# Streaming both halves of the activations in one 512-column matmul, and a new order of the first layer's projections

## The chip, the cores and the metric

The kernel runs on one core of one Trainium2 chip. The metric is the device time of one execution in microseconds (us); "before" and "after" are compared as medians of several executions. TensorE (PE) multiplies, ScalarE (ACT) and VectorE (DVE) prepare operands and drain results, GpSimd (POOL) and SyncE (SP) issue transfers.

## The reference, cut to what matters

The input is `x` of 256 rows by 2048 columns in float32. Three layers follow each other:

```python
h = rmsnorm(x, attn_norm[0]); p = h @ even_w_in[0]        # 2048 x 6144
qa, ka, va, qb, kb, vb = split(p, 6 * [1024])
# A: 8 heads of 128, relative-position bias;  B: 4 heads with two maps each, out = (p0 - lam * p1) @ v, rmsnorm
x = x + concat(A, B) @ even_w_out[0];  x = x + ffn(rmsnorm(x), 0)
h = rmsnorm(x, attn_norm[1]); p = h @ odd_w_in[0]          # queries 2048, latent 256, index queries 512, index key 64, 8 weights
# C: index scores pick 64 keys per row; 16 heads attend over them through the latent
x = x + C @ odd_w_out[0];  x = x + ffn(rmsnorm(x), 1)
# third layer: a convolution branch, windowed attention, gates, w_out_2, layer norm
```

All of it is float32. The products are made with float32r operands split in two: a high part (a rounded copy) and a low part (the rest). Of the four partial products three are computed: high x high, high x low, low x high.

## The kernel before, in words

**Units and groups.** Every weight matrix is read in *units* of 512 KB (4 tiles of 128 rows by 256 columns, or 2 tiles by 512 columns in a "wide" unit). For each unit SP issues one transfer into a ring of four buffers `raw`; ACT makes the high part (`hi`, L190, instruction L195), DVE the low part (`lo`, L197, instruction L201), both into `ws`; PE multiplies. Some units make a *group*, which accumulates into two PSUM banks of `PG`; groups alternate between banks 0,1 and banks 2,3. `Seg` (L42) numbers units and groups of a stage. The semaphore `s_mm` counts finished units, `s_drain` drained groups.

**Three ways to multiply a unit.** `mul_T` (L215) gives transposed results: the weights are stationary and the activations `hs` (high part at `[.., 0, :]`, low part at `[.., 1, :]`, 256 columns each, side by side in memory) stream; a unit is 4 x 2 triples of 256-column matmuls, 24 instructions, all recorded at L223. Queries, keys and the index products of the second layer use it. `mul_N` (L227) gives natural results: the activations are stationary, 256 columns of weights stream; 24 instructions at L234. The values of the first layer and one group of the third use it. `mul_W` (L238) does the same with 512 columns of weights in a wide unit: 12 instructions at L245. Everything else uses it.

**Who does what in which order.** There is no scheduler. `group_pe` (L248) is PE's side of a group: it waits for the bank (`s_drain`), then for each unit waits for `lo`, multiplies, and after unit j runs `hooks[j]`. `group_side` (L264) is the side of ACT and of DVE: for each unit j the hook `("early", j)`, at the last unit the drain of the group, then `hi` or `lo` for the unit four places ahead (which waits until PE has finished unit j), then the hook j. Attention is spread over these hooks by hand, so each engine runs a fixed list, and a wait in it holds back all that is behind it on that engine.

**The first layer.** `even` (L870) is called for A (`gA`) and B (`gBs`), each 12 groups of 4 units: for each of four pairs j of heads a query group, a key group (both `mul_T`) and a value group (`mul_N`). The steps of pair j run in the hooks of the next three groups (`hooks`, L955): scores `S_` on PE (L791, L792), `max_` on DVE (`maxima`, L795, instructions L806 to L809), `exps` on ACT (L817), `soft` on DVE (L890; A: L827, B: L894 to L902), the turn `T_` on PE (L834), `pt_` on ACT (L845), the product with the values `V_` on PE (L854, L855). B goes on with `b_sq` (ACT, L919), `b_st` (PE, L923 and L924), `b_a` (DVE, L615), `rstd_act` (ACT), `b_on` (DVE, L626 to L629 and L932), `b_hi` (ACT, L937) and `b_lo` (DVE, L943). The steps of B's last pair run in the hooks of the first group of the output projection `gEO` (L1013). Its last units wait for B's last tiles.

**Drains.** `scaled_drain` (L371) is one DVE instruction (L377, or L381 where the rows are turned round) from PSUM, scaled by 1/rms, into `qst`, `kst` or `qi`.

**The second layer.** `gI` (L1088) has four groups: index key, latent, two of index queries; `score` (L1040) on PE follows from its fourth group on, `c_norm` (L1126) on DVE lies in the third. `gU` (L1157) makes keys and values from the latent; `gQ` (L1277) makes the 16 heads' queries in eight groups of 4 units. Over `gU` and the first groups of `gQ` DVE runs eight rounds of `top` (L1061), then `selection`; POOL then adds the masks, DVE does `c_max`, ACT `exps`, DVE `norms` (L827), and PE's `flips` (L834) of the first heads come after the first unit of `gQ`'s third group.

Of the kernel before, what the change touches and what calls it, by code (L numbers as in the profile page):

```python
# [30 lines left out]
UK = 4  # L31
# [37 lines left out]
def build(nc, a):  # L69
# [30 lines left out]
    vst1 = at("vst1", [P, 2, S], F32, o1 + 49152 + 1536)  # L100
    cs = at("cs", [P, 2, 2, S], F32R, o1 + 53248)
# [395 lines left out]
    def setup_act(e):  # L497
# [16 lines left out]
        w(e, "nat", 1)  # L514
# [198 lines left out]
    def ffn(p, seg, segd, l, before_seg, norm, own, pn, gain):  # L713
# [4 lines left out]
        cross_before = {"f0": 0, "f1": 19}[p]  # L718
# [130 lines left out]
    def mix(e, p, j, v, free, pt=lambda h: pT[:, h, :]):  # L849

        w(e, p + "pT", j + 1)
        free()
        for h in (0, 1):
            e.matmul(PO[:, h, 0:S], v(0, h), pt(h)[:, 0:S], start=True, stop=False)  # L854
            ins = e.matmul(PO[:, h, P:S], v(1, h), pt(h)[:, S:384], start=False, stop=True)  # L855
        ins.then_inc(sem(p + "O"), 1)
# [13 lines left out]
    def even(seg, p, c0, before):  # L870

        is_b = p == "B"
        k_of = [0, 1]

        def S_(e, pp, j):
            sg = gA if pp == "A" else gBs
            if pp == "B":
                w(e, "BD", 5 * j)
            scores(e, pp, j, lambda h: qst[:, 0, h, :], lambda h: kst[:, h, :],
                   lambda: e.wait_ge(s_drain, sg.group(0, 3 * j + 1) + 3))  # L880
# [52 lines left out]

        def b_hi(e, j):
            w(e, "Bon", j + 1)
            for h in (0, 1):
                e.activation(os_[:, bass.ds(8 + 2 * j + h, 1), 0, :], sqb[:, h:h + 1, :], ACT.Copy, scale=gB[:, h:h + 1]).then_inc(sem("Boh"), 1)  # L937

        def b_lo(e, j):
            w(e, "Boh", 2 * j + 2)  # L940
            for h in (0, 1):
                t = bass.ds(8 + 2 * j + h, 1)
                e.scalar_tensor_tensor(os_[:, t, 1, :], sqb[:, h:h + 1, :], gB[:, h:h + 1], os_[:, t, 0, :].bitcast(F32), ALU.mult, ALU.subtract).then_inc(sem("Bos"), 1)  # L943

        def start_hooks(name, e):

            return {k: hooked(e, v) for k, v in {
                "pe": {0: {0: lambda e: (x_pe(e, 2), tables_pe(e)), 1: lambda e: x_pe(e, 3)}, 1: {0: lambda e: (w(e, "tabD", 3), spread_pe(e, "n0"))}, 2: {1: lam_pe}},
                "act": {0: {0: lambda e: squares(e, "n0", 3), 1: lambda e: norm_act(e, "n0")}, 2: {2: lam_act}},
                "dve": {0: {0: lambda e: (norm_first(e, "n0"), lines_second(e)), 1: lambda e: (norm_second(e, "n0"), spread_diag(e, "n0")),  # L950
                            ("late", 3): lambda e: spread_copy(e, "n0")},
                        2: {3: lambda e: lam_dve(e)}}}[name].items()}


        def hooks(name, e, pp, j):  # L955
            A = {"pe": {0: {0: lambda: S_(e, pp, j)}, 1: {0: lambda: T_(e, pp, j), 2: lambda: V_(e, pp, j)}},
                 "act": {0: {1: lambda: exps(e, pp, j)}, 1: {0: lambda: pt_(e, pp, j), 3: lambda: out_hi(e, pp, j, 2 * j)}},
                 "dve": {0: {0: lambda: max_(e, pp, j), 2: lambda: soft(e, pp, j)}, 1: {3: lambda: out_lo(e, pp, j, 2 * j)}}}
            B = {"pe": {0: A["pe"][0], 1: A["pe"][1], 2: {0: lambda: b_st(e, j)}},
                 "act": {0: A["act"][0], 1: {0: lambda: pt_(e, pp, j), 2: lambda: b_sq(e, j)},  # L960
                         2: {0: lambda: rstd_act(e, "B", j), 3: lambda: b_hi(e, j)}},
                 "dve": {0: A["dve"][0], 2: {("early", 1): lambda: b_a(e, j), 1: lambda: b_on(e, j), 3: lambda: b_lo(e, j)}}}
            return (A if pp == "A" else B)[name]
# [1022 lines left out]
```

## Time and profile before

| | |
|---|---|
| median of 3 executions | 2540.35 us (2539.18 to 2540.77) |
| the profiled execution, its own time | 2539.02 us |
| its span, first to last instruction | 2536.8 us |
| PE busy | 2512.4 us, 99%, 13171 matmuls |
| DVE busy | 1441.6 us, 57% |
| ACT busy | 1181.5 us, 47% |
| mean granted TensorE clock | 0.998 |
| read from HBM | 459.63 MB, 182 GB/s over the span |

The profile page gives the busy time of each engine, the span in 40 slices, the chain of work that ended last and the costliest groups of instructions. Matmuls overlap in the pipeline, so the "mean ns of one" of a matmul is longer than its share of the time; the share is read from the chain, where a run of n matmuls has its duration. The time outside the span is 2539.02 - 2536.8 = 2.2 us.

### The profile page before, as it was taken

To read this page: it belongs to the slowest core of one execution; us is meant where nothing else is said; L and a number is where in the kernel's file an instruction comes from. 1 tells how busy PE (TensorE), PEld (TensorE's weight loads), DVE (VectorE), ACT (ScalarE), POOL (GpSimd) and SP (SyncE) were. 2 spreads that over 40 slices of the span, in tenths; PEclk is the share of its full clock that TensorE was granted. 3 is DMA by queue.
4 is the path that set the end of the run, shared out by engine and by line. 5 is a ranking of instruction groups with operands and counts; after the bars stand their busy time and mean duration, and the time that the engine had idled before them with its cause. 6 is when DMAs were issued, how large, how long until landed. Compare 5 with 4: busy or idle time off the path is not lost.

```text
span 2536.8 us, 34992 instructions
## 1 busy us (share of the span) xinstructions
PE 2512.4 (99%) x13171; PEld 2154.9 (85%) x13171; DVE 1441.6 (57%) x1967; ACT 1181.5 (47%) x1543; POOL 50.1 (2%) x71
## 2 busy tenths in 40 slices
PE   9999999999999999999999999999999999999997
PEld 9999988888888888889998888888888888888776
DVE  6555555544544544446765554554554444798875
ACT  5344455444444444444444544444444444545763
POOL 1000000000000000000120000000000000000000
PEclk9999999999999999999999999999999999999999
DMA  7555555656556655546544566656655555655453
GB/s 230 171 171 171 166 174 181 194 189 189 188 189 187 189 191 191 191 167 208 162 142 168 179 195 189 188 187 190 189 189 192 190 191 191 219 183 162 147 181 133
DMA packets 291477, 463.31 MB, mean 183 GB/s; under 512 B 17343, under 2 KB 115825, under 8 KB 290858
## 3 DMA queue, kind: packets, MB, share of 16 engines
q1 hardware_dynamic: 288960, 453.63, 55.1%
q0 software_dynamic: 1792, 8.11, 1.0%
q8 instruction: 73, 1.20, 0.2%
q14 instruction: 34, 0.28, 0.0%
q10 hardware_dynamic: 618, 0.09, 0.0%
HBM read 459.63 MB, written 2.14 MB: 182 GB/s over the span
## 4 chain that ended last, share of the span: by engine, by line
PE 95%; DVE 2%; ACT 2%; issue 1%; DMA 0%; DVEq 0%; SPq 0%; ACTq 0%
PE PG L245 73%; PE PG L223 12%; PE PG L234 4%; PE PS L729 1%; DVE ws L201 1%; PE PS L568 1%; PE PS L791 1%; PE PO L854 1%; ACT ws L195 1%; PE PS L834 0%; PE PG L1170 0%; PE PO L1179 0%; DVE cacc L1401 0%; PE PO L855 0%; PE PS L792 0%
## 5 line engine op out<-in xcount | busy, mean ns | idle before, releaser
L201 DVE TENSOR_TENSOR ws<-raw,ws 128x1024 fp32r<-128x1024 f32 x860 | 1055.8, 1229 | 1022.4 <-ACT ws L195 1018.0
L195 ACT ACTIVATE ws<-raw 128x1024 fp32r<-128x1024 f32 x860 | 910.3, 1060 | 1206.5 <-PE PG L245 948.0
L245 PE MATMUL PG<-ws,hs 128*128 128x512 f32 x5184 | 1191.3, 390 | 0.0
L245 PEld LDWEIGHTS PG<-ws,hs 128*128 128x128 f32 x5184 | 969.2, 188 | 200.5
L245 PE MATMUL PG<-ws,fs 128*128 128x512 f32 x2112 | 481.3, 389 | 0.0
L245 PEld LDWEIGHTS PG<-ws,fs 128*128 128x128 f32 x2112 | 395.9, 188 | 81.9
L223 PE MATMUL PG<-hs,ws 128*128 128x256 f32 x2640 | 331.3, 285 | 0.4 <-issue 0.3
L223 PEld LDWEIGHTS PG<-hs,ws 128*128 128x128 f32 x2640 | 320.7, 192 | 1.9 <-issue 1.0
L245 PE MATMUL PG<-ws,os 128*128 128x512 f32 x1152 | 267.9, 392 | 2.0 <-DVE ws L201 1.3
L245 PEld LDWEIGHTS PG<-ws,os 128*128 128x128 f32 x1152 | 214.7, 188 | 47.9 <-DVE ws L201 3.2
L234 PE MATMUL PG<-ws,hs 128*128 128x256 f32 x864 | 106.6, 284 | 0.0
L234 PEld LDWEIGHTS PG<-ws,hs 128*128 128x128 f32 x864 | 104.9, 192 | 0.2
L1401 DVE SCALAR_TENSOR_TENSOR cacc<-hc,convw,cacc 128x256 f32<-128x256 f32 x232 | 98.0, 479 | 0.0
L817 ACT ACTIVATE ts<-ts,small 128x256 f32<-128x256 f32 x96 | 42.4, 443 | 23.4 <-DVE small L809 23.4
L757 ACT ACTIVATE cross<-PG,small 128x512 f32<-128x512 f32 x44 | 27.9, 686 | 33.2 <-PE PG L245 33.2
L770 DVE SCALAR_TENSOR_TENSOR qst<-PG,small,cross 128x512 f32<-128x512 f32 x44 | 31.0, 747 | 10.5 <-PE PG L245 10.5
L559 DVE SCALAR_TENSOR_TENSOR hs<-PS,gains,hs 128x256 fp32r<-128x256 f32 x72 | 29.8, 477 | 4.3 <-ACT hs L552 4.3
L552 ACT ACTIVATE hs<-PS,gains 128x256 fp32r<-128x256 f32 x72 | 28.0, 471 | 5.8 <-PE PS L585 5.8
L738 DVE TENSOR_TENSOR fs<-PS,fs 128x1024 f32 (+1 forms) x22 | 26.8, 1218 | 0.0
L545 ACT ACTIVATE cross<-x 128x512 f32<-128x512 f32 x40 | 25.3, 634 | 2.9 <-DVE x L708 0.3
L729 PEld LDWEIGHTS PS<-ident,qst 128*128 128x128 f32 x176 | 20.5, 140 | 2.9
L708 DVE TENSOR_TENSOR x<-x,PG 128x1024 f32<-128x1024 f32 x16 | 19.5, 1220 | 5.9 <-PE PG L245 5.9
(264 smaller groups left out, 832.0 us busy)
## 6 DMA issues: line engine op xcount, KB each, us to landing
raw<-in_w_gate SPq DMA_DIRECT2D x176, 512.0 KB, 4.3
raw<-in_w_up SPq DMA_DIRECT2D x176, 512.0 KB, 3.5
raw<-in_w_down SPq DMA_DIRECT2D x176, 512.0 KB, 3.4
raw<-in_even_w_in SPq DMA_DIRECT2D x96, 512.0 KB, 3.5
raw<-in_w_in SPq DMA_DIRECT2D x52, 512.0 KB, 3.4
raw<-in_odd_w_in SPq DMA_DIRECT2D x44, 512.0 KB, 3.5
raw<-in_even_w_out SPq DMA_DIRECT2D x32, 512.0 KB, 3.5
raw<-in_odd_w_out SPq DMA_DIRECT2D x32, 512.0 KB, 3.4
```

Source lines behind the costliest of these rows:

```text
L195: e.activation(ws[j % RING][:, :, 0, :], raw[:, j % RING], ACT.Copy).then_inc(s_hi, 1)
L201: e.tensor_tensor(w[:, :, 1, :], raw[:, j % RING], w[:, :, 0, :].bitcast(F32), ALU.subtract).then_inc(s_lo, 1)
L223: ins = e.matmul(PG[:, bank + c, 0:S], w_, x_, start=first and kk == 0 and n == 0, stop=last and kk == UK - 1 and n == 2)
L234: ins = e.matmul(PG[:, bank + b, 0:UC], x_, w[:, kk, h, :], start=first and kk == 0 and n == 0, stop=last and kk == UK - 1 and n == 2)
L245: ins = e.matmul(out[:, b, :], x_, w[:, kk, :, h, :], start=first and kk == 0 and n == 0, stop=last and kk == 1 and n == 2)
L552: e.activation(hs[:, n, 0, :], src(t), ACT.Copy, scale=gains[:, gain, n:n + 1]).then_inc(sem(p + "hi"), 1)
L559: e.scalar_tensor_tensor(hs[:, n, 1, :], src(t), gains[:, gain, n:n + 1], hs[:, n, 0, :].bitcast(F32), ALU.mult, ALU.subtract).then_inc(se ...
L729: ins = e.transpose(turned[:, t, b * P:(b + 1) * P], nat_f[:, b, t * P:(t + 1) * P], ident[:])
L757: ins = e.activation(sil[:, b], gates[:, b, :], ACT.Silu, scale=rnT[:, b:b + 1])
L770: ins = e.scalar_tensor_tensor(nat_f[:, b], ups[:, b, :], rnT[:, b:b + 1], sil[:, b], ALU.mult, ALU.mult)
L817: e.activation(ts[:, h, src], ts[:, h, src], ACT.Exp, bias=nmx[:, n:n + 1], accum_out=sm[:, n:n + 1]).then_inc(sem(p + "e"), 1)
L1401: e.scalar_tensor_tensor(dst, hc[:, n, c:c + S], convw[:, n, c:c + 1], dst, ALU.mult, ALU.add).then_inc(sem("cv"), 1)
```

## The change

It has five parts.

1. `mul_T` streams high and low part of the activations together: per tile and column block one matmul of 512 columns with the high weights, one of 256 columns with the low weights, in place of three of 256.
2. The high x low part now lies in columns 256 to 511 of the bank. So the drain of such a group is three steps: ACT copies these columns to `cross` (`crossing`), DVE adds the other half (`summed`), DVE scales as before. This holds for the first layer's queries and keys, for `gI` and for `gQ`.
3. The values of the first layer are made by `mul_W`, two pairs of heads in one group of 8 wide units, into a new buffer `vab`; `mul_N` stays in the third layer.
4. The order of the groups in A and B is now a string, and the hooks are written out anew (`steps`). B's last value group comes behind all keys, and B's pairs 2 and 3 are finished in the hooks of `gEO`, with statistics in other places of PSUM.
5. PE no longer waits for the drain of `gI`'s last group ahead of `gU`; counts of `s_cross` are adapted.

```diff
 def mul_T(e, bank, j, k0, rhs, first, last, tiles=(0, 1)):
...
-                xh, xl = (rhs[:, k0 + kk, h, :] for h in (0, 1))
-                for n, (w_, x_) in enumerate(((wh, xh), (wh, xl), (wl, xh))):
-                    ins = e.matmul(PG[:, bank + c, 0:S], w_, x_, start=first and kk == 0 and n == 0,
-                                   stop=last and kk == UK - 1 and n == 2)
+                both = rhs[:, k0 + kk].rearrange("p h s -> p (h s)")
+                st, end = first and kk == 0, last and kk == UK - 1
+                if not st:
+                    e.matmul(PG[:, bank + c, 0:S], wl, rhs[:, k0 + kk, 0, :], start=False, stop=False)
+                ins = e.matmul(PG[:, bank + c, :], wh, both, start=st, stop=end)
+                if st:
+                    ins = e.matmul(PG[:, bank + c, 0:S], wl, rhs[:, k0 + kk, 0, :], start=False, stop=False)
...
-    gA = Seg(1, [4] * 12, [0, 2] * 6)
-    gBs = Seg(1, [4] * 12, [0, 2] * 6)
+    gA = Seg(1, [4, 4, 8, 4, 4, 4, 4, 8, 4, 4], [0, 2] * 5)
+    gBs = Seg(1, [4, 4, 8, 4, 4, 4, 4, 4, 4, 8], [0, 2] * 5)
...
+    def crossing(e, seg, i, k, m=2):
+
+        q = seg.banks[k]
         e.wait_ge(s_mm, seg.end(i, k) + RING)
-        c = halves(seg, k, m)
+        e.activation(cross[:, q // 2, 0:m], PG[:, q:q + m, S:2 * S], ACT.Copy).then_inc(s_cross, 1)
+
+    def scaled_drain(e, seg, i, k, dst, crossed, n, scale=1.0, turned=None):
+
+        m, q = dst.shape[1], seg.banks[k]
+        c = cross[:, q // 2, 0:m]
+        e.wait_ge(s_cross, crossed + n + 1)
+        e.tensor_tensor(c, PG[:, q:q + m, 0:S], c, ALU.add).then_inc(sem("summed"), 1)
+        e.wait_ge(sem("summed"), n + 1)
...
+        order_of = {"A": "QKVQKQKVQK", "B": "QKVQKQKQKV"}
+        at_k = {"A": (1, 4, 6, 9), "B": (1, 4, 6, 8)}
+        at_v = {"A": (2, 7), "B": (2, 9)}
...
+            def narrow(pp, j, g, u=0):
+                put(e, at, {"pe": {(g, u): lambda: S_(e, pp, j), (g + 1, u): lambda: T_(e, pp, j), (g + 1, 2): lambda: V_(e, pp, j)},
+                            "act": {(g, 1): lambda: exps(e, pp, j), (g + 1, 0): lambda: pt_(e, pp, j)},
+                            "dve": {(g, 0): lambda: max_(e, pp, j), (g, 2): lambda: soft(e, pp, j)}}[name])
+
+            def broad(pp, j, g):
+                put(e, at, {"pe": {(g, 1): lambda: S_(e, pp, j), (g, 5): lambda: T_(e, pp, j), (g + 1, 1): lambda: V_(e, pp, j)},
+                            "act": {(g, 2): lambda: exps(e, pp, j), (g, 5): lambda: pt_(e, pp, j)},
+                            "dve": {(g, ("early", 2)): lambda: max_(e, pp, j), (g, 3): lambda: soft(e, pp, j)}}[name])
...
+            if not is_b:
...
+                broad("A", 0, 2)
+                out("A", 0, 3, 2)
+                narrow("A", 1, 5)
+                out("A", 1, 6, 3)
+                broad("A", 2, 7)
+                out("A", 2, 8, 2)
+                return at
+            narrow("A", 3, 0)
+            out("A", 3, 1, 3)
+            broad("B", 0, 2)
+            put(e, at, {"pe": {(3, 2): lambda: b_st(e, 0)},
+                        "act": {(3, 1): lambda: b_sq(e, 0), (3, 3): lambda: rstd_act(e, "B", 0), (4, 1): lambda: b_hi(e, 0)},
+                        "dve": {(3, 2): lambda: b_a(e, 0), (4, 0): lambda: b_on(e, 0), (4, 2): lambda: b_lo(e, 0)}}[name])
+            narrow("B", 1, 5)
+            put(e, at, {"pe": {(7, 0): lambda: (b_st(e, 1), S_(e, "B", 2)), (8, 0): lambda: T_(e, "B", 2), (9, 1): lambda: S_(e, "B", 3)},
+                        "act": {(6, 2): lambda: b_sq(e, 1), (7, 0): lambda: rstd_act(e, "B", 1), (7, 2): lambda: exps(e, "B", 2), (7, 3): lambda: b_hi(e, 1),
+                                (8, 0): lambda: pt_(e, "B", 2), (9, 2): lambda: exps(e, "B", 3)},
+                        "dve": {(7, ("early", 1)): lambda: b_a(e, 1), (7, 1): lambda: (b_on(e, 1), max_(e, "B", 2)), (7, 3): lambda: (soft(e, "B", 2), b_lo(e, 1)),
+                                (9, ("early", 2)): lambda: max_(e, "B", 3), (9, 3): lambda: soft(e, "B", 3)}}[name])
+            return at
...
     residual(gEO, a["even_w_out"][0], os_, "n1", 2, lambda e: (lambda j: w(e, "Bos", 2 * j - 6) if j > 3 else w(e, "Aos", j + 1)),
...
+             {0: lambda e: (f["T"](e, "B", 3), f["V"](e, "B", 2)), 1: lambda e: (f["st"](e, 2), f["V"](e, "B", 3)), 2: lambda e: f["st"](e, 3)},
+             {0: lambda e: (f["sq"](e, 2), f["pt"](e, "B", 3)), 1: lambda e: (f["sq"](e, 3), rstd_act(e, "B", 2)), 2: lambda e: (f["hi"](e, 2), rstd_act(e, "B", 3)),
+              4: lambda e: f["hi"](e, 3)},
+             {("early", 1): lambda e: f["a"](e, 2), 1: lambda e: f["on"](e, 2), ("early", 2): lambda e: f["a"](e, 3), 2: lambda e: f["lo"](e, 2),
+              3: lambda e: (f["on"](e, 3), f["lo"](e, 3))})
...
-        e.wait_ge(s_drain, gI.group(0, 3) + 3)
```

In the new tables a key (g, u) means: group g of this stage, hook of unit u; Q, K and V are the groups in order.

## Rows read from the trace of the kernel before

**Rows 1.** the page: busy time of each engine; the TensorE clock granted, 40 slices

```profile
PE 2512.4 (99%) x13171; PEld 2154.9 (85%) x13171; DVE 1441.6 (57%) x1967; ACT 1181.5 (47%) x1543; POOL 50.1 (2%) x71
...
PEclk9999999999999999999999999999999999999999
```

**Rows 2.** matmul groups by form: count | busy us, mean ns | idle

```profile
L223 PE MATMUL PG<-hs,ws 128*128 128x256 f32 x2640 | 331.3, 285 | 0.4 <-issue 0.3
...
L234 PE MATMUL PG<-ws,hs 128*128 128x256 f32 x864 | 106.6, 284 | 0.0
```

**Rows 3.** chain that ended last, 231 to 375 us: start us, us, what

```profile
231.29 0.43 PE PS L923 x2
...
232.16 8.63 PE PG L234 x72
...
243.67 0.43 PE PS L791 x2
...
244.98 11.52 PE PG L223 x96
...
352.87 21.79 PE PG L245 x96
```

**Rows 4.** timeline of PE at the start: start, us, what [idle before it]

```profile
30.12 0.67 PE L677 MATMUL PO<-na,ones 128*128 128x256 f32 x2 [1.00 <-DVE na L672]
```

**Rows 5.** groups by form of DVE and ACT: count | busy us, mean ns

```profile
L864 DVE TENSOR_TENSOR os<-PO,os 128x512 f32 x6 | 4.1, 683 | 0.0
...
L1199 ACT ACTIVATE kC<-PG 128x512 f32<-128x512 f32 x4 | 2.4, 598 | 7.7 <-PE PG L1170 7.7
```

**Rows 6.** timeline of ACT and DVE in B: start us, us, what

```profile
231.39 1.06 ACT L195 ACTIVATE ws<-raw 128x1024 fp32r<-128x1024 f32 x1 [1.82 <-PE PG L234]
...
232.48 1.23 DVE L201 TENSOR_TENSOR ws<-raw,ws 128x1024 fp32r<-128x1024 f32 x1 [1.65 <-ACT ws L195]
...
246.01 0.42 DVE L806 CUSTOM_DVE_ANT_0 ts<-PS,biasM 128x256 f32<-128x256 f32 x1
...
247.24 0.17 DVE L809 TENSOR_SCALAR small<-small 128x4 f32<-128x4 f32 x1
...
248.92 0.49 ACT L817 ACTIVATE ts<-ts,small 128x256 f32<-128x256 f32 x1
...
250.83 1.06 ACT L195 ACTIVATE ws<-raw 128x1024 fp32r<-128x1024 f32 x1
...
253.07 0.17 DVE L894 RECIPROCAL small<-small 128x4 f32<-128x4 f32 x1
...
254.73 0.68 DVE L381 SCALAR_TENSOR_TENSOR qst<-PG,rn 128x512 f32<-128x512 f32 x1
```

**Rows 7.** timeline of DVE in the third group of gI

```profile
1174.02 1.23 DVE L201 TENSOR_TENSOR ws<-raw,ws 128x1024 fp32r<-128x1024 f32 x1 [2.18 <-ACT ws L195]
1175.16 0.42 DVE L626 TENSOR_TENSOR nt<-na,ny 128x256 f32<-128x256 f32 x1
...
1177.47 0.68 DVE L381 SCALAR_TENSOR_TENSOR qi<-PG,rn 128x512 f32<-128x512 f32 x1
```

**Rows 8.** chain that ended last, 1178 to 1246 us

```profile
1178.58 0.63 PE PS L1046 x2
...
1217.97 17.38 PE PG L223 x144
...
1245.30 0.84 PE PS L834 x6
```

**Rows 9.** timeline of DVE ahead of the first flips in gQ

```profile
1243.57 1.64 DVE L827 TENSOR_SCALAR ts<-ts,small 128x256 f32<-128x256 f32 x4
```

**Rows 10.** timeline of PE at the last unit of gEO's first group

```profile
340.84 11.16 PE L245 MATMUL PG<-ws,os 128*128 128x512 f32 x48 [0.31 <-DVE os L943]
```

**Rows 11.** chain that ended last, first 16 us: two runs of eight transposes

```profile
5.09 1.97 PE PS L585 x8
...
14.82 0.87 PE PS L585 x8
```

More of the change, by code:

```diff
@@ L853, in mix @@
         for h in (0, 1):
[L854 to L855 removed]
+            e.matmul(PO[:, h, c:c + S], v(0, h), pt(h)[:, 0:S], start=True, stop=False)
+            ins = e.matmul(PO[:, h, c + P:c + S], v(1, h), pt(h)[:, S:384], start=False, stop=True)
         ins.then_inc(sem(p + "O"), 1)
@@ L951, in start_hooks @@
                             ("late", 3): lambda e: spread_copy(e, "n0")},
[L952 to L963, printed above, removed]
+                        1: {2: lambda e: lam_dve(e)}}}[name].items()}
@@ L1006, in stage, with weights @@
                     even_bias(e, h + n, 1 if h + n > 7 else 2)
-        phase(sp=stream(seg, lambda i, k, j: cols(W, j, c0 + 1024 * (k % 3) + UC * (k // 3)), begun=0 if is_b else 4), pe=run("pe"), act=run("act"), dve=run("dve"), pool=stage)
-        return hooks, {"S": S_, "max": max_, "T": T_, "soft": soft, "pt": pt_, "V": V_, "sq": b_sq, "st": b_st, "a": b_a, "on": b_on, "hi": b_hi, "lo": b_lo}
-    even(gA, "A", 0, None)
-    _, f = even(gBs, "B", 3072, "A")
-    residual(gEO, a["even_w_out"][0], os_, "n1", 2, lambda e: (lambda j: w(e, "Bos", 2 * j - 6) if j > 3 else w(e, "Aos", j + 1)),
-             {2: lambda e: f["T"](e, "B", 3), 3: lambda e: f["V"](e, "B", 3), 4: lambda e: f["st"](e, 3)},
-             {("early", 1): lambda e: exps(e, "B", 3), 2: lambda e: f["pt"](e, "B", 3), 3: lambda e: f["sq"](e, 3),
-              4: lambda e: (rstd_act(e, "B", 3), f["hi"](e, 3))},
-             {("early", 0): lambda e: f["max"](e, "B", 3), ("early", 1): lambda e: f["soft"](e, "B", 3), ("early", 4): lambda e: (f["a"](e, 3), f["on"](e, 3), f["lo"](e, 3))})
+        def weights(e):
+            for g, kind in enumerate(order_of[p]):
+                n = order_of[p][:g].count(kind)
+                for j in range(seg.groups[g]):
+                    if kind == "V":
+                        load(e, seg, 0, seg.first(g) + j, wide_cols(W, j, c0 + 2048 + 2 * UC * n), 1)
+                    elif is_b or g:
+                        load(e, seg, 0, seg.first(g) + j, cols(W, j, c0 + 1024 * (kind == "K") + UC * n))
@@ new lines, in even @@
+        phase(sp=weights, pe=run("pe"), act=run("act"), dve=run("dve"), pool=stage)
+        return {"S": S_, "max": max_, "T": T_, "soft": soft, "pt": pt_, "V": V_, "sq": b_sq, "st": b_st, "a": b_a, "on": b_on, "hi": b_hi, "lo": b_lo}
+    even(gA, "A", 0)
+    f = even(gBs, "B", 3072)
+    residual(gEO, a["even_w_out"][0], os_, "n1", 2, lambda e: (lambda j: w(e, "Bos", 2 * j - 6) if j > 3 else w(e, "Aos", j + 1)),
+             {0: lambda e: (f["T"](e, "B", 3), f["V"](e, "B", 2)), 1: lambda e: (f["st"](e, 2), f["V"](e, "B", 3)), 2: lambda e: f["st"](e, 3)},
[3 more added lines that the diff above has]
+              3: lambda e: (f["on"](e, 3), f["lo"](e, 3))})
```

134 lines of the change are left out of this document (78 added, 56 removed).

## The prediction

> **What bounds the kernel now.** I read the page first. PE is busy 99% of the span and its granted clock is full in all 40 slices [rows 1], so time falls only where PE streams for less time, and every wait that PE newly takes comes straight on top. Next the groups by form: 2640 matmuls at L223 and 864 at L234, 256 columns wide, with almost no idle time before them [rows 2]. Their mean durations overlap in the pipeline and are no price; the price is in the chain. There 96 matmuls of 256 columns take 11.52 us and 72 take 8.63 us, 119.9 ns each; 96 of 512 columns take 21.79 us, 227.0 ns each [rows 3]. Two narrow ones cost 239.8 ns, so one wide in their place saves 12.8 ns. This is the whole gain that the change can have on PE.
>
> **What the wide matmuls save.** A triple in `mul_T` (359.7 ns) becomes 227.0 + 119.9 = 346.9 ns. L223 holds 2640 / 3 = 880 triples, which is 110 units of 24 instructions; a unit falls from 2.88 to 2.77 us. 880 x 12.8 ns = 11.3 us. Of the 864 at L234, 96 stay (the third layer's one group of four units); 768 become 384 wide ones, 384 x 12.8 ns = 4.9 us, a unit falling to 2.72 us. Sum 16.2 us. The mixture of 512 and 256 is not in the trace. Its bounds: a pair can't be cheaper than the two streams (346.9 ns, unless the fixed part shrinks too), and with no saving it stays at 359.7 ns. I take 346.9, because the extra over the bare columns is alike at both widths. The Trainium skill (TensorE: Matmul & The Clock Gate, "Back-to-back issue gap") puts the fixed part of a warm matmul at about 2.5 ns; by that, as an estimate from the page, 1264 saved instructions would bring 3.2 us instead of 16.2. The rows show about 13 ns each, and I go by them.
>
> **The start.** PE idles 1.00 us at 30.12 us until DVE has made the diagonal [rows 4]; that DVE chain hangs on the last turn of `x`, two units earlier. The three units between are shortened for nothing: 3 x 0.10 = -0.3 us.
>
> **The longer drain.** ACT's copy costs 0.60 us and DVE's sum 0.68 us [rows 5], the scaling 0.68 us as before [rows 7]. ACT and DVE are busy 47% and 57% [rows 1]; 24 groups (16 in the first layer, 8 in `gQ`) plus four in `gI` add 17 us to ACT and 19 us to DVE, hidden except where a result is due soon. From a group's end to its result it is now about 0.1 + 0.60 + 0.03 + 0.68 + 0.03 + 0.68 = 2.1 us instead of 0.75. Where scores follow after one unit (A's pairs 1 and 3, B's 1 and 2) PE comes at 2.77 us: 0.6 us spare, nothing. `gOO` and `gQ` read their queries later than that: nothing. Ahead of `gU` the old wait would now cost about 1 us, but part 5 takes it away, and the score that needs the result comes one unit later: nothing. The banks come free a whole group ahead.
>
> **gI.** `c_norm` keeps DVE before the third group's drain. That group's unit 2 ends at 1178.58 - 2 x 2.88 = 1172.83 us [rows 8]; DVE starts `c_norm` at 1175.16 and the drain at 1177.47 [rows 7], 4.64 us after it. Sum and scaling end 4.64 + 0.71 + 0.71 = 6.06 us after it, PE wants to score after two units, 5.55 us: -0.5 us.
>
> **gQ.** PE's nine units from 1217.97 to 1245.30 (17.38 us are six of them, and three follow the scores) run beside DVE's rounds of `top`. The first flips take 0.84 us where others take 0.66 [rows 8], so PE already waits 0.18 us: DVE's `norms` start at 1243.57 and last 1.64 us, to 1245.21 [rows 9]. I count that DVE is the bound from the first `top` on, through `selection`, POOL's masks and `c_max`. Then PE comes 9 x 0.10 = 0.93 us earlier, and DVE 0.71 us later (one sum in this stretch). The nine units' gain is lost and 0.71 us on top: -1.6 us.
>
> **The new order in B.** The steps of the first seven groups keep at least two units between `soft` and the turn that needs it. Pair 2 doesn't: `soft` lies behind unit 3 of group 7, `T_` behind unit 0 of group 8. Walk, with 0 where PE ends unit 0 of group 7. PE: `b_st` 0.87 and scores 1.31 (differences of the starts in [rows 3]), then units to 4.95, 7.73, 10.50 and 13.28 us; there it wants to turn. DVE: `lo` starts 1.19 us after a unit's end [rows 3, 6], its next step 1.14 us later [rows 7]; so `b_on` starts at 7.28 and takes 2.31 as `c_norm`, the same steps, does [rows 7]. `max_` runs 9.59 to 11.01 (1.42), then ACT's `exps` 1.91 to 12.92 [rows 6]. All this holds up ACT's copy for group 7: to 13.52; DVE's sum and scaling to 14.91; its `lo` to 16.05; `soft` 1.66 [rows 6] and about 0.1 until the flag: 17.8. PE waits 4.5 us. Even with nothing held up, copy, `hi` (1.06), `lo` and `soft` after 10.50 end at about 15.1: the bounds are 1.8 and 4.5 us, and I take -4.4. Behind it nothing is late: ring and banks have two units in hand.
>
> **gEO.** PE waits 0.31 us for B's last tiles now [rows 10]. In the new tables `b_st` of pair 3 comes at unit 2 instead of 4; by the same durations the last `b_lo` ends about 1.6 us before unit 7. +0.3 us. `T_`, `V_` and `b_st` only change places. Transfers: units come as fast as in the wide stages, which run without idle PE.
>
> **Sum.** 16.2 - 0.3 - 0.5 - 1.6 - 4.4 + 0.3 = 9.7 us. The span of 2536.8 becomes 2527.1, the profiled execution of 2539.0 becomes 2529.3; the median stands 1.3 us above that execution, and I apply the difference to it: 2540.35 - 9.7 = 2530.6 us.
>
> **Rivals.**
> (a) *The turn's wait is short*, because `max_` or `b_on` runs earlier than in my walk. It saves up to 4.4 us: about 2526.5. Against it: the lists are in order, and 1.8 us is the least. Chance 0.10.
> (b) *The clock falls in the long wait.* Now no slice shows less than the full clock, with PE busy 99% of the time [rows 1]; a wait of over 4 us is new. At the start it ran at its lower level, 1.2 instead of 2.4 GHz: eight transposes took 1.97 us, later 0.87 us [rows 11]. That is over half of the time lost while it lasts; it lasted less than the 10 us between the two rows, so the price is 0 to 4.9 us, about 2.5: 2533. The Trainium skill (TensorE: Matmul & The Clock Gate, "Part 1: The HAM clock gate") says that idle time throttles the clock back until activity releases it, which speaks against this order. Chance 0.15.
> (c) *More handoffs wait.* The spare 0.6 us at four score hooks is thin, and POOL or a late transfer can eat it; at 1 us each in all four, 2534.6. Chance 0.10.
> (d) *Mixed widths save nothing* in `mul_T` (359.7 ns a triple), only the values gain: 4.9 us against waits of 6.5 us, which shrink by the 1.2 us that PE then doesn't come earlier at the start and in `gQ`; 2540.7. Against it: both pure widths show the same fixed part. Chance 0.05.
> (e) *Slower: the low weights' load is exposed.* The high weights of a pair can only be loaded behind 256 columns, the low ones behind 512; if alternating breaks this overlap, a pair costs more than the triple did. It decides from 346.9 + 9.7 / 0.88 = 358 ns a pair (no gain left) and 364 ns (slower by 0.2%); at 20 ns more than the triple it is 2540.35 + 17.6 - 4.9 + 4.6 (the waits without those of `gQ` and the start) = 2557.7. Against it: 2640 matmuls with a load each stand at 119.9 ns behind 256 columns [rows 2, 3]. Chance 0.04.
> That the change doesn't do what it says has no room: it is in the instructions. My forecast has the remaining 0.56.
>
> **How the numbers follow.** The forecast's own range is 2528.5 to 2532.5, from the waits' sizes. With (a), (b) and most of (c) it is 2525.5 to 2535.5; (d), (e) and the worst of (c) are left out, with some of what I have overlooked. What a measurement can tell from no change is 0.2%, 5.1 us: faster is below 2535.3. That takes the forecast, (a), (b) and most of (c): 0.87. Same: the rest of (c) and (d): 0.09. Slower: (e): 0.04.
>
> **What would show it.** Chain: a unit of `mul_T` of 16 instructions in 2.77 us, of the values 12 in 2.72 us. PE's waits: about 4.4 us at L834 in B for DVE's `soft`, 0.5 us at the first score in the fourth group of `gI`, 1.8 us at the first flips of `gQ`, none in `gEO`'s first group. The granted clock just behind the 4.4 us tells (b). A pair at 360 ns or more, or units' times alike with long idle elsewhere, would make the prediction wrong.

## The result, and the profile after

The change makes the kernel faster, by less than was predicted. Before: 2539.74 us, median of 15 runs; after: 2533.51 us (2532.62 to 2535.35, 15 runs), ratio 0.9976 [0.9968, 0.9984]. That is 6.2 us less, where 9.7 us was predicted (2530.6); the time lies in the range given (2525.5 to 2535.5), but not in the forecast's own (2528.5 to 2532.5). The profiled execution took 2532.88 us, its span 2531.0 us; before they were 2539.02 and 2536.8 us.

The page after, against [rows 1]:

```profile
PE 2499.5 (99%) x11907; PEld 2086.8 (82%) x11907; DVE 1458.8 (58%) x1987; ACT 1194.4 (47%) x1571; POOL 50.0 (2%) x71
...
PEclk9999999999999999999999999999999999999999
```

PE is still the bound, with 1264 matmuls less, and a fortieth of the span is too coarse to show a short fall of the clock. The matmul groups by form (count | busy us, mean ns | idle), against [rows 2]:

```profile
L249 PE MATMUL PG<-ws,hs 128*128 128x512 f32 x5568 | 1281.1, 390 | 0.0
...
L226 PE MATMUL PG<-hs,ws 128*128 128x512 f32 x880 | 309.1, 395 | 0.5 <-issue 0.5
...
L225 PE MATMUL PG<-hs,ws 128*128 128x256 f32 x825 | 235.9, 286 | 0.3 <-DVE hs L567 0.2
```

880 wide and 825 narrow matmuls (and 55 more narrow ones at L228) stand where 2640 narrow ones were; the values have joined the wide ones of L249. The waits of PE (total us, times, longest):

```profile
PE PS L842 <- DVE ts L910: 4.4, 1, 4.4
PE PO L598 <- POOL ident L412: 2.0, 1, 2.0
PE PS L1805 <- ACT csq L1814: 1.9, 1, 1.9
PE PS L842 <- DVE ts L835: 1.4, 1, 1.4
...
PE PO L685 <- DVE na L680: 1.1, 1, 1.1
PE PS L1119 <- DVE qi L389: 0.6, 1, 0.6
```

4.4 us at pair 2 of B, 1.4 us at the first flips of `gQ`, 0.6 us at the first score of `gI`. The other three were there before, at 1.8, 1.9 and 1.0 us. The wait of `gEO` [rows 10] is gone. The chain that ended last shows how the long wait is made (start us, us, what):

```profile
267.45 1.07 ACT ws L196
...
269.76 0.35 DVE nt L634
...
273.85 1.45 ACT ts L825 x7
275.30 0.49 ACT cross L375
...
275.81 0.70 DVE cross L382
...
276.54 0.69 DVE qst L389
...
279.28 0.76 DVE ts L910 x2
...
280.09 0.90 PE PS L842 x3
...
281.21 0.43 PE PG L226
...
283.08 0.23 PE PG L226
```

DVE's `b_on` (from L634), ACT's seven `exps` (L825), then the new drain (L375, L382, L389), a rounding of weights and `soft` (to L910) follow each other, and only then can PE turn at 280.09. Behind the wait a wide matmul takes 0.43 us in the chain, from 283.08 on 0.23: PE runs at half its clock. The stretches of 4 us around it (length, PE busy (count), granted clock, DMA share, GB/s) say the same:

```profile
276.00:280.00 4.00, 0.00 (x0) 0.94 0.48 140
280.00:284.00 4.00, 3.91 (x17) 0.64 0.50 154
284.00:288.00 4.00, 4.00 (x25) 1.00 0.24 91
```

**Where PE stands at three places.** With the spread matmul at 30.12 us [rows 4], two places of the kernel before (timeline of PE), the first transposes of `x` in `gEO` and the first product behind `gQ`:

```profile
397.18 1.03 PE L568 MATMUL PS<-ident,x 128*128 128x128 f32 x8
...
1331.88 3.01 PE L245 MATMUL PG<-ws,os 128*128 128x512 f32 x12
```

and the same three after:

```profile
30.52 0.67 PE L685 MATMUL PO<-na,ones 128*128 128x256 f32 x2 [1.11 <-DVE na L680]
...
393.31 1.03 PE L576 MATMUL PS<-ident,x 128*128 128x128 f32 x8
...
1326.30 3.01 PE L249 MATMUL PG<-ws,os 128*128 128x512 f32 x12
```

The start has lost 0.40 us. From there to `gEO` PE needs 362.79 us instead of 367.06: 4.27 less. From there to the end of `gQ` 932.99 instead of 934.70: 1.71 less. Behind that 0.22 us less. The sum, 5.8 us, is the difference of the spans. Five units, 40 pairs, stand ahead of the first place. So by the prediction's own terms these were 0.2 (the first two of the five; the other three were counted as lost), 6.8 (472 triples of the 512, the values, the turn, `gEO`) and 2.6 us (368 triples, `gI`, `gQ`). So most of what is missing is missing in the first layer.

### The profile page after: what moved, and what is told of

It reads as the page before. It is cut to its first block, busy times and chain, and to the rows that moved or that the text cites. A ratio compares the mean times of both kernels' runs of the same rounds, so it can differ in the third digit from the quotient of the medians.

```text
span 2531.0 us, 32535 instructions
## 1 busy us (share of the span) xinstructions
PE 2499.5 (99%) x11907; PEld 2086.8 (82%) x11907; DVE 1458.8 (58%) x1987; ACT 1194.4 (47%) x1571; POOL 50.0 (2%) x71
## 4 chain that ended last, share of the span: by engine, by line
PE 93%; DVE 4%; ACT 2%; issue 1%; DMA 0%; DVEq 0%; SPq 0%; ACTq 0%
PE PG L249 77%; PE PG L226 7%; PE PG L225 3%; DVE ws L202 1%; PE PS L737 1%; ACT ws L196 1%; PE PS L576 1%; PE PO L862 1%; PE PS L799 1%; PE PS L842 1%; PE PG L238 0%; DVE cacc L1476 0%; PE PG L1247 0%; DMA x<-in_x 0%; PE PS L800 0%
## 5 line engine op out<-in xcount | busy, mean ns | idle before, releaser
L249 PE MATMUL PG<-ws,hs 128*128 128x512 f32 x5568 | 1281.1, 390 | 0.0
L249 PEld LDWEIGHTS PG<-ws,hs 128*128 128x128 f32 x5568 | 1040.8, 188 | 215.2
L249 PE MATMUL PG<-ws,fs 128*128 128x512 f32 x2112 | 481.3, 389 | 0.0
L249 PEld LDWEIGHTS PG<-ws,fs 128*128 128x128 f32 x2112 | 395.9, 188 | 81.9
L226 PE MATMUL PG<-hs,ws 128*128 128x512 f32 x880 | 309.1, 395 | 0.5 <-issue 0.5
L249 PE MATMUL PG<-ws,os 128*128 128x512 f32 x1152 | 267.5, 391 | 1.7 <-DVE ws L202 1.3
L249 PEld LDWEIGHTS PG<-ws,os 128*128 128x128 f32 x1152 | 214.8, 188 | 47.3 <-DVE ws L202 3.3
L225 PE MATMUL PG<-hs,ws 128*128 128x256 f32 x825 | 235.9, 286 | 0.3 <-DVE hs L567 0.2
L825 ACT ACTIVATE ts<-ts,small 128x256 f32<-128x256 f32 x96 | 42.4, 443 | 27.2 <-DVE small L817 27.2
L375 ACT ACTIVATE cross<-PG 128x512 f32<-128x512 f32 (+1 forms) x28 | 16.5, 588 | 40.2 <-PE PG L226 40.2
L382 DVE TENSOR_TENSOR cross<-PG,cross 128x512 f32<-128x512 f32 (+1 forms) x28 | 19.1, 681 | 21.1 <-ACT cross L375 21.0
```

The source lines that it names most:

```text
L225: e.matmul(PG[:, bank + c, 0:S], wl, rhs[:, k0 + kk, 0, :], start=False, stop=False)
L226: ins = e.matmul(PG[:, bank + c, :], wh, both, start=st, stop=end)
L249: ins = e.matmul(out[:, b, :], x_, w[:, kk, :, h, :], start=first and kk == 0 and n == 0, stop=last and kk == 1 and n == 2)
L825: e.activation(ts[:, h, src], ts[:, h, src], ACT.Exp, bias=nmx[:, n:n + 1], accum_out=sm[:, n:n + 1]).then_inc(sem(p + "e"), 1)
```

## The experiments

Twelve kernels were run. The first four change one thing in the kernel after. With the first one's result known, the others take that one (`e1_turn_later`) as their base. One diff stands for each; stages and landmarks are those above.

### 1. The turn two hooks later

```diff
-put(e, at, {"pe": {(7, 0): lambda: (b_st(e, 1), S_(e, "B", 2)), (8, 0): lambda: T_(e, "B", 2), (9, 1): lambda: S_(e, "B", 3)},
+put(e, at, {"pe": {(7, 0): lambda: (b_st(e, 1), S_(e, "B", 2)), (8, 2): lambda: T_(e, "B", 2), (9, 1): lambda: S_(e, "B", 3)},
...
-                    (8, 0): lambda: pt_(e, "B", 2), (9, 2): lambda: exps(e, "B", 3)},
+                    (8, 2): lambda: pt_(e, "B", 2), (9, 2): lambda: exps(e, "B", 3)},
```

> The changed kernel, with the turn of B's pair 2 on PE and its copy on ACT behind unit 2 instead of unit 0 of group 8. Theory (the 4.4 us wait at L842 and the 3.4 us at half clock behind it are both caused by the early turn): no wait over 0.5 us at L842 in B, full clock up to the tail, and 4.4 + 1.6 = 6.0 us less than the changed kernel's 2533.5, so 2527.5. Rival 1 (the clock would have fallen anyway, or fell by chance): 4.4 us less, 2529.1. Rival 2 (DVE's backlog only moves the wait on to the next thing that it feeds): a new wait at the weights or the next scores, and 2531 or more.

2527.47 us (5 runs), ratio 0.9951 [0.9937, 0.9965]. Timeline of PE at the three places, and the stretch of 280 to 284 us:

```profile
30.39 0.67 PE L685 MATMUL PO<-na,ones 128*128 128x256 f32 x2 [0.91 <-DVE na L680]
...
387.25 1.03 PE L576 MATMUL PS<-ident,x 128*128 128x128 f32 x8
...
1320.26 3.00 PE L249 MATMUL PG<-ws,os 128*128 128x512 f32 x12
```

```profile
280.00:284.00 4.00, 4.00 (x26) 1.00 0.49 160
```

From the start to `gEO` 356.86 us, 5.93 less than after; the rest is alike (933.01 us to the end of `gQ`). The wait of L842 for L910 isn't in this kernel's list, and the clock stays full. The turn's place costs 5.9 us in the profile and 6.0 by the medians, more than its wait of 4.4 us.

### 2. The wait filled with work

```diff
-put(e, at, {"pe": {(7, 0): lambda: (b_st(e, 1), S_(e, "B", 2)), (8, 0): lambda: T_(e, "B", 2), (9, 1): lambda: S_(e, "B", 3)},
+put(e, at, {"pe": {(7, 0): lambda: (b_st(e, 1), S_(e, "B", 2)), (8, 0): lambda: (w(e, "Bmx", 12), [e.transpose(PS[:, 1, 384:512], ident[:], ident[:]) for _ in range(36)], T_(e, "B", 2)), (9, 1): lambda: S_(e, "B", 3)},
```

> The changed kernel, with 36 transposes of the identity on PE (36 x 0.109 = 3.9 us, into an unused part of PS) ahead of the early turn of B's pair 2. The turn still waits for DVE until the same time, but PE is not idle meanwhile. Theory (the idle wait makes the clock fall, and that costs 1.6 us): the turn starts as late as before, full clock behind it, 2533.5 - 1.6 = 2531.9. Rival 1 (the clock falls for another reason): half clock stays, 2533.5. Rival 2 (the clock costs nothing, PE catches up): 2533.5 with full clock.

2532.37 us (7 runs), ratio 0.9970 [0.9959, 0.9981]. Timeline of PE, and the stretch:

```profile
275.47 4.09 PE L1015 MATMUL PS<-ident 128*128 128x128 f32 x36
...
280.04 0.55 PE L842 MATMUL PS<-ident,ts 128*128 128x128 f32 x3 [0.47 <-DVE ts L910]
...
391.96 1.03 PE L576 MATMUL PS<-ident,x 128*128 128x128 f32 x8
```

```profile
280.00:284.00 4.00, 3.96 (x24) 1.00 0.50 160
```

The turn starts where it started after (280.04 against 280.09 us), but three transposes take 0.55 instead of 0.90 us and the clock is full. From the start (30.48 us) to `gEO` it needs 361.48 us, 1.31 less than after. The medians say 1.1 us. This is the price of the fallen clock alone; the wait with the clock held is the remaining 4.6 us. Rival 1, a fall for another reason, is out: with PE busy in the same stretch the clock stays up. So is rival 2: with the clock full the time is shorter.

### 3. and 4. Three narrow matmuls again; values in 256 columns again

```diff
-                if not st:
-                    e.matmul(PG[:, bank + c, 0:S], wl, rhs[:, k0 + kk, 0, :], start=False, stop=False)
-                ins = e.matmul(PG[:, bank + c, :], wh, both, start=st, stop=end)
                 if st:
-                    ins = e.matmul(PG[:, bank + c, 0:S], wl, rhs[:, k0 + kk, 0, :], start=False, stop=False)
+                    e.matmul(PG[:, bank + c, :], wh, both, start=True, stop=False)
+                elif not end:
+                    e.matmul(PG[:, bank + c, 0:S], wh, both[:, 0:S], start=False, stop=False)
+                    e.matmul(PG[:, bank + c, S:2 * S], wh, both[:, S:2 * S], start=False, stop=False)
+                ins = e.matmul(PG[:, bank + c, 0:S], wl, both[:, 0:S], start=False, stop=False)
+                if end:
+                    ins = e.matmul(PG[:, bank + c, :], wh, both, start=False, stop=True)
```

> The changed kernel with three matmuls of 256 columns in mul_T again, where the accumulation's first and last pair allow it (14 of 16 pairs, 770 of 880), all else as changed: same drains, same order. Theory (one wide matmul saves 12.8 ns against two narrow ones, also mixed with narrow ones): 770 x 12.8 = 9.9 us more PE time, less 0.9 us that the flips of gQ then wait less and 0.3 us at the start: 2533.5 + 8.7 = 2542.2. Rival (mixed widths save less: the pairs measured 350.5 ns on average in the first layer, 9.2 ns saved): 770 x 9.2 = 7.1, less 0.9: 2539.7. Rival 2 (the wide form saves nothing): 2533.5.

2540.74 us (11 runs), ratio 1.0003 [0.9994, 1.0012]: 7.2 us over after, between the theory (2542.2) and the first rival (2539.7).

```diff
-                        group_pe(e, seg, 0, g, W_mul(hs) if kind == "V" else T_mul(hs), hk,
+                        group_pe(e, seg, 0, g, W_mul_halves(hs) if kind == "V" else T_mul(hs), hk,
...
+                        for m in (0, 1):
+                            ins = e.matmul(PG[:, bank + b, m * S:(m + 1) * S], x_, w[:, kk, m, h, :], start=False, stop=False)
```

> The changed kernel with the first layer's values in 256-column matmuls again (46 of 48 per bank: 368 of the 384 wide ones are split in two), in the new groups, units and order. Theory: 368 x 12.8 = 4.7 us more, 2538.2. Rival (the gain of the values came from the wide transfers or the fewer drains, not from the width): 2533.5.

2537.57 us (11 runs), ratio 0.9990 [0.9981, 0.9999]: 4.1 us over after, so the rival (no cost of the width) is out. The last of the three stretches, in this kernel:

```profile
284.00:288.00 4.00, 4.00 (x15) 0.55 0.47 142
```

The clock stays down longer than after (there it is full again over this whole stretch), with the same wait of 4.4 us; in kernel 3, whose wait of 4.1 us ends at 284.1 us, it is 0.50 over 284 to 288 us and 0.76 over the next 4 us. So neither difference is a clean price of the width. They are taken again without the wait in 10 and 11.

### 5. Wide matmul first in each pair

```diff
-                if not st:
-                    e.matmul(PG[:, bank + c, 0:S], wl, rhs[:, k0 + kk, 0, :], start=False, stop=False)
-                ins = e.matmul(PG[:, bank + c, :], wh, both, start=st, stop=end)
-                if st:
-                    ins = e.matmul(PG[:, bank + c, 0:S], wl, rhs[:, k0 + kk, 0, :], start=False, stop=False)
+                e.matmul(PG[:, bank + c, :], wh, both, start=st, stop=False)
+                ins = e.matmul(PG[:, bank + c, 0:S], wl, rhs[:, k0 + kk, 0, :], start=False, stop=end)
```

> The kernel with the later turn, with the wide matmul ahead of the narrow one in every pair of mul_T (the changed kernel has the narrow one first but for the first pair of a group). In its trace the pairs of the first layer take 347 ns in some stretches and 353 ns in others, always from the values' group to the next scores or statistics. Theory A (the narrow-first order sets the slow stretches off): all pairs at 347 ns, about 190 slow pairs x 6.6 ns = 1.3 us less than 2527.5: 2526.2. Theory B (what came before the stretch sets it off, whatever the order): the same stretches, 2527.5.

2528.85 us (5 runs), ratio 0.9959 [0.9945, 0.9972], 1.4 us over its base: neither theory. From the start to the first product behind `gQ` its profile needs 1292.06 us, 2.2 more than the base's 1289.87. The starts of the wide matmuls tell why. The first and the fourteenth of an undisturbed row, twice in the kernel after and once in this one:

```profile
250.27 0.39 PE L226 MATMUL PG<-hs,ws 128*128 128x512 f32 x1
...
254.78 0.39 PE L226 MATMUL PG<-hs,ws 128*128 128x512 f32 x1
```

```profile
137.58 0.40 PE L226 MATMUL PG<-hs,ws 128*128 128x512 f32 x1
...
142.16 0.40 PE L226 MATMUL PG<-hs,ws 128*128 128x512 f32 x1
```

```profile
137.44 0.40 PE L224 MATMUL PG<-hs,ws 128*128 128x512 f32 x1
...
142.04 0.40 PE L224 MATMUL PG<-hs,ws 128*128 128x512 f32 x1
```

After has two paces. Most rows go at 347 ns, as the first one does (4.51 / 13); those behind a group of values, as the second (4.58 / 13 = 352 ns a pair), at 352 to 353, and so do a few others (at 34, 1150 and 1232 us). With the wide one first (4.60 / 13 = 354) most rows stand at 353 to 354, though some stay at 347 (at 265 and 1209 us). So theory B fails, and theory A had the order the wrong way round. The order in the change is the better one, and the pace isn't the sum of the two widths alone.

### 6. The first sum of gQ left out

```diff
-        e.tensor_tensor(c, PG[:, q:q + m, 0:S], c, ALU.add).then_inc(sem("summed"), 1)
+        if seg is gQ and k == 0 and isinstance(i, int):
+            e.sem_inc(sem("summed"), 1)
+        else:
+            e.tensor_tensor(c, PG[:, q:q + m, 0:S], c, ALU.add).then_inc(sem("summed"), 1)
```

> The kernel with the later turn, without DVE's sum in the drain of gQ's first group (so the low part of the first two heads' queries is left out of the result). PE waits 1.4 us there for DVE's norms at the first flips. Theory (DVE is the bound from the first round of top to the first flips, so the sum is paid in full): the wait falls from 1.4 to 0.7 us, 2526.8. Rival (DVE has room in that stretch, PE's faster units alone make the wait): 1.4 us stays, 2527.5.

2526.74 us (5 runs), ratio 0.9947 [0.9934, 0.9961], 0.7 us under its base. The wait of PE:

```profile
PE PS L845 <- DVE ts L838: 0.5, 1, 0.5
```

It was 1.4 us. From the start to the first product behind `gQ` the profile needs 1289.17 us, 0.70 less than the base. DVE is the bound up to the first flips, and one sum of 0.69 us lies on that path. (Without the sum the low part of the first two heads' queries is missing from the result.)

### 7. and 8. The norm behind the drain; a clearing on POOL

```diff
-hk = ({("early", 0): lambda: rows_hi(e, "n2", 3, 1), 0: lambda: norm_act(e, "n2")}, {2: kic}, {0: square_c, 2: lambda: rstd_act(e, "c"), 3: c_hi}, {j: (lambda j=j: relu(e, j)) for j in range(4)})[k]
+hk = ({("early", 0): lambda: rows_hi(e, "n2", 3, 1), 0: lambda: norm_act(e, "n2")}, {2: kic}, {0: square_c, 2: lambda: rstd_act(e, "c")}, {0: lambda: (relu(e, 0), c_hi()), 1: lambda: relu(e, 1), 2: lambda: relu(e, 2), 3: lambda: relu(e, 3)})[k]
...
-hk = ({("early", 0): lambda: (norm_first(e, "n2"), rows_lo(e, "n2", 3, 1)), 0: lambda: (norm_second(e, "n2"), spread_diag(e, "n2"))}, {0: clear}, {1: c_mean, 2: c_norm},
+hk = ({("early", 0): lambda: (norm_first(e, "n2"), rows_lo(e, "n2", 3, 1)), 0: lambda: (norm_second(e, "n2"), spread_diag(e, "n2"))}, {0: clear}, {1: c_mean, 3: c_norm},
```

> The kernel with the later turn, with c_norm on DVE behind the drain of gI's third group and c_hi on ACT behind the first unit of its fourth. Theory (c_norm ahead of the now longer drain makes PE wait 0.6 us for qi at the first score): no wait there, 2526.9. Rival (the latent's high and low parts now come too late for gU, or the scores wait for ACT): a new wait at L1247 or L1119, 2527.5 or more.

2526.30 us (5 runs), ratio 0.9946 [0.9932, 0.9959], 1.2 us under its base by the medians; the wait at L1119 is gone.

```diff
         e.tensor_scalar(selm[:], sc, LOWEST / 1.5, NEG, ALU.is_gt, ALU.mult).then_inc(sem("sel"), 1)
-        w(e, "biasC", 16)
-        e.memset(biasC[64:P, :, 192:256], NEG).then_inc(sem("sel"), 1)
...
     def c_pool(e):
+        w(e, "biasC", 16)
+        e.memset(biasC[64:P, :, 192:256], NEG).then_inc(sem("sel"), 1)
```

> The kernel with the later turn, with the memset of biasC (0.9 us, with 0.27 us ahead of it) moved from DVE, between the last round of top and the masks, to POOL, which is idle then. Theory (the chain top, selection, masks, c_max, exps, norms bounds the first flips of gQ): the chain is 1.1 us shorter, the wait of 1.4 us falls to 0.3: 2526.4. Rival (POOL's masks and DVE's two slow lo instructions set it): the wait stays at 1.4, 2527.5.

2526.20 us (5 runs), ratio 0.9945 [0.9932, 0.9959], 1.3 us under its base. The wait at the first flips is gone. One of 1.1 us for rounded weights has come; the timeline of PE puts it at the start:

```profile
12.09 0.47 PE L226 MATMUL PG<-hs,ws 128*128 128x512 f32 x1 [1.10 <-DVE ws L202]
```

So it has nothing to do with the clearing: the first weights are late there where in other kernels `x` is. The expectation of kernel 9 still counts on it, but in 9 it isn't there; PE waits 1.2 us for `x` instead.

### 9. and 12. All three together, and the base once more

9 has the edits of 7 and of 8 on the base of 1; 12 is kernel 1 unchanged.

> All the stalls that the change opened are taken out together: the keys' turn put behind (as in e1_turn_later), the norm's last piece behind the drain (as in e7_norm_behind_drain) and one clearing on POOL (as in e8_memset_on_pool). Theory (the gains add, since each is a wait of TensorE at another place): 2527.5 less 1.2 (e7: 2526.30 against 2527.5) less 1.3 (e8: 2526.20) gives 2525.0, with no wait of TensorE above 1 us in the first layer but the start and the 1.1 us on the weights that e8_memset_on_pool showed. Rival (each piece's work only moves along the same queue, so that the gains overlap): 2526.2, no better than the better of the two.

> The same kernel as e1_turn_later, as the base for the three runs beside it. Both theories: 2527.5, from 2526.8 to 2528.2.

9: ratio 0.9945 [0.9932, 0.9958], median 2525.95 us of five executions; a sixth took 11190.3 us and is left out of both. 12: 2527.52 us (5 runs), ratio 0.9950 [0.9937, 0.9963], the base as before. So the medians say 1.6 us, between the theory's 2.5 and the rival's 1.3. The profiles say more. The first product behind `gQ`, in 12, 7, 8 and 9:

```profile
1320.21 3.01 PE L249 MATMUL PG<-ws,os 128*128 128x512 f32 x12
```

```profile
1319.54 3.01 PE L249 MATMUL PG<-ws,os 128*128 128x512 f32 x12
```

```profile
1319.05 3.01 PE L249 MATMUL PG<-ws,os 128*128 128x512 f32 x12
```

```profile
1318.37 3.01 PE L249 MATMUL PG<-ws,os 128*128 128x512 f32 x12
```

(Their starts, the place at 30 us, lie within 0.13 us.) Against 12 they are 0.67, 1.16 and 1.84 us earlier, and 0.67 + 1.16 = 1.83. The gains add, as the theory had it; its sizes, taken from medians (1.2 and 1.3), were too large, the first above all. The rival is out. No kernel run is faster than this one: 13.9 us under the runs of before beside it (2539.86).

12 shows one more thing. It is the same program as 1, but PE is 1.7 us later in it by 2430 us. The same stretch of the third layer, in 1 and in 12:

```profile
2424.00:2428.00 4.00, 4.00 (x20) 1.00 0.22 80
```

```profile
2424.00:2428.00 4.00, 4.00 (x14) 0.67 0.23 82
```

At or behind the wait of 1.9 us at L1805, which all these kernels have, the clock fell in the profiled execution of 12 and not in that of 1; 0.9 us of it is left in the span (2525.9 against 2525.0). It fell in the profiles of 3, 6, 7, 8, 9 and 12, and not in those of before, after, 1, 2, 4, 5, 10 and 11. That is how two executions of one program can differ by a microsecond.

### 10. and 11. The prices of the widths, with no long wait

Their edits are those of 3 and of 4, on the base of 1.

> The 770 triples of queries, keys and index products in three narrow matmuls each (as in e3_three_narrow), but with the keys' turn put behind, so that there is no long wait in which the clock could fall. Theory (a merged matmul saves what the rows of before gave, 12.8 ns): 770 x 12.8 = 9.9 us more, less 0.9 us of the queries' first sum that comes earlier and less 0.3 us at the start, over the 2527.5 of e1_turn_later: 2536.2. Rival (the pairs at 353 ns in place of 347 take the mean saving to some 9 ns): 770 x 9.2 = 7.1, less 0.9: 2533.7. The clock stays whole in both.

2534.53 us (11 runs), ratio 0.9979 [0.9970, 0.9988], 7.0 us over its base, nearer the rival (2533.7) than the theory (2536.2). Timeline of PE at the start and behind `gQ`:

```profile
30.68 0.67 PE L688 MATMUL PO<-na,ones 128*128 128x256 f32 x2 [1.05 <-DVE na L683]
...
1327.56 3.01 PE L252 MATMUL PG<-ws,os 128*128 128x512 f32 x12
```

1296.88 us between the two, 1289.87 in the base: 7.0 us more, though PE's wait at the first flips fell from 1.4 to 0.8. That makes 7.6 us for the 736 of the 770 triples that lie there, 10.3 ns each. So the 12.8 ns of the rows of before are out as the mean of all pairs.

> The values in 256 columns again (368 matmuls of 512 columns split in two, as in e4_values_narrow), with the keys' turn put behind. Theory (a matmul of 256 columns that is not merged costs 12.8 ns, as in the rows of before): 368 x 12.8 = 4.7 us over 2527.5: 2532.2. Rival (11 ns, as e4_values_narrow gave beside the other stall): 2531.6. If the clock's fall behind the long wait was what differed there, the clock is whole here.

2530.88 us (5 runs), ratio 0.9965 [0.9952, 0.9978], 3.4 us over its base, less than either had it (4.7 and 4.1 us). Timeline of PE, the start and `gEO`, then the same row of pairs as in 5:

```profile
30.39 0.67 PE L701 MATMUL PO<-na,ones 128*128 128x256 f32 x2 [0.86 <-DVE na L696]
...
139.32 0.40 PE L226 MATMUL PG<-hs,ws 128*128 128x512 f32 x1
...
143.84 0.39 PE L226 MATMUL PG<-hs,ws 128*128 128x512 f32 x1
...
390.95 1.03 PE L592 MATMUL PS<-ident,x 128*128 128x128 f32 x8
```

From the start to `gEO` 360.56 us, 3.70 over the base: 10.1 ns for each of the 368 matmuls split. But this row of pairs, behind a group of values, now goes at 4.52 / 13 = 348 ns instead of 352. So the narrow values give something back: the starts of the wide matmuls of the first layer lie 347.7 ns apart on average (gaps of 300 to 400 ns, those from pair to pair), in the base 349.3. That is 1.6 ns less on the 472 pairs behind the start, 0.75 us. The values' own price is then (3.7 + 0.75) / 368 = 12.1 ns, close to the rows of before; where the values are wide, the pairs behind them pay a part of this back.

## Why the prediction was right, and where it was off

**The number** came out in the range partly by luck. The forecast itself stood at 2528.5 to 2532.5 us; 2533.51 is close to rival (b)'s 2533, but (b) put the whole distance down to a fallen clock, and the runs give the clock half of it. The rest is above all the pair's price.

**What bounds the kernel** was read rightly: each wait and each saved matmul of PE came straight on the time. Point by point, in the order of the prediction, by the profile:

- *Wide matmuls in `mul_T`*: 11.3 us predicted, 12.8 ns a triple. This is the term that was mis-sized most. Kernel 10 measured 10.3 ns: 9.1 us. The sum of the two streams, 346.9 ns, was taken as what a pair takes; it is the best pace that any row shows, and behind a group of values a pair takes 352. The mean of the first layer, 349.3 ns, agrees with the triple's 359.7 less 10.3. The mixture wasn't in the trace of before, and its bound below was used as its value. The Trainium skill (TensorE: Matmul & The Clock Gate, "Back-to-back issue gap") has about 2.5 ns as the fixed part of a warm matmul; by that, as an estimate from the page, the 770 split triples of kernel 10 would have cost 1.9 us. The run doesn't agree: 7.0 us.
- *Values*: 4.9 us predicted, 12.8 ns each; 12.1 ns by kernel 11, 4.6 us. A unit of the new kernel takes 10.94 / 4 = 2.735 us in its chain, predicted 2.72:

```profile
46.59 10.94 PE PG L249 x48
```

- *The start*: the gain of three units was counted as lost, that of two as won, so the place at 30.12 us should have come 0.2 us earlier; it is 0.40 us later. PE waits 2.0 us instead of 1.8 for POOL's diagonal (in every kernel with the change: the diagonal is now made behind another clearing). But the chain of this execution runs through a transfer of `x` that lands at 9.42 us, and the place varies from 30.10 to 30.79 us over the kernels with that same diagonal. So no run shows what the 0.2 us at the diagonal costs.
- *The longer drain* hidden where the walk said so: no new wait at the other scores. Rival (c) didn't come.
- *`gI`*: 0.5 us predicted, 0.6 measured, 0.67 won by kernel 7 (with the wait gone).
- *`gQ`*: 1.6 us predicted, a wait of 1.8 in all; 1.4 measured. DVE is the bound there, as kernels 6 and 8 show.
- *The turn of pair 2*: a wait of 4.5 us by the walk, 4.4 in the sum, 4.4 measured, and the chain above is the walk of the prediction, step by step. Rival (a), a shorter wait, is out. (Its price, up to 4.4 us, did not fit the walk's own lower bound of 1.8 us.)
- *`gEO`*: 0.3 us predicted; its wait is gone.
- *Rival (b)*, the clock falls in the long wait, was given 0.15 and happened, beside the forecast's waits. Its price was put at about 2.5 us; kernel 2 measures 1.3 (1.1 by the medians). The Trainium skill (TensorE: Matmul & The Clock Gate, "Part 1: The HAM clock gate") says that idle time throttles the clock back; the trace agrees, 0.64 over 280 to 284 us behind the wait and 1.00 at the same place when transposes fill it.
- *Rivals (d) and (e)* are out: the widths pay, and no row of pairs comes near 358 ns.

From the start to `gEO` the measured terms make 472 x 10.3 ns = 4.9, plus 4.6, less 4.4, less 1.3, plus 0.3: 4.1 us; PE gained 4.27. Behind it 368 x 10.3 ns = 3.8, less 0.6, less 1.2 (the wait of 1.4 less the 0.2 of before): 2.0 us; PE gained 1.71. These differences, 0.2 and 0.3 us, stay without a name.

So the direction, the places of the waits and nearly all their lengths were right. Of the 3.5 us that the medians miss, the step that failed is above all the pair's price (2.2 us), then the clock, which the sum left out (1.3), the start (0.6) and the values (0.3). `gQ`, what lies behind it, and the time around the span gave about one microsecond back. Of the 12 us that a placement without stalls brings (kernel 1, 12.5 us under before), half was given away by one hook that stands two units too early.

Not settled: what makes a pair take 347 or 352 ns. Kernel 5 shows that the order within a pair decides it nearly everywhere, kernel 11 that the width of the values ahead decides it for the row behind them; neither shows what in the array or its queue is late. The 15 runs of after lie in two groups, 2532.6 to 2533.8 and 2534.3 to 2535.4 us, and kernels 3 and 4 had the clock down longer than the profiled execution of after. The mean granted clock of each execution supports this: it is 0.996 in all six of the upper group and 0.997 in eight of the nine of the lower. But no profile of an upper one was taken, so where its clock was down is not shown.

## What to carry to other kernels

When matmuls are merged, a mixture of widths that the trace doesn't show may cost more than the sum of its streams; take that sum as the bound, not as the value. Here a fifth of the gain stayed out. When an order is written anew, walk every engine's queue from the producer to the hook that needs it: one hook two units too early cost half of the gain here, and moving it cost nothing. A wait of some microseconds on TensorE can cost its length and the slow clock behind it, here 4.6 and 1.3 us.

## What the runs showed of the hardware

- Pairs of 256 and 512 columns go at 347 or at 352 to 354 ns, steady over a row. The same pairs change pace with the order inside the pair (kernel 5) and with the width of the matmuls ahead of the row (kernel 11).
- The clock fell in every wait of 4.1 to 4.4 us (after, 3, 4) and was still down when PE went on. When 36 transposes filled the wait it stayed full, and what followed ran at full speed. Behind a wait of 1.9 us it fell in some executions and not in others of the same program (1 and 12).
- Two profiles of one program agree closely: in 1 and 12 the three places stand within 0.06 us, so differences of 0.1 us in a stage can be read, while the medians of five runs put kernel 7 at 1.2 us where its profile shows 0.67.
